# Tokens of the normalised input moved to multiples of 128 bytes, and a 272/256 split of two sections, in a hybrid decoder block on one core

## What is computed

```python
u = rmsnorm(h, norm_g[l])
proj = jnp.einsum('bld,de->ble', u, w_in[l])
hq, hf, hi, hz, aq, ak, av, az, ga, gb = jnp.split(proj, offs, axis=-1)
```

```python
yA = jnp.einsum('blw,wd->bld', oA * jax.nn.silu(hz), w_branch_a[l])
yB = jnp.einsum('blw,wd->bld', oB * jax.nn.silu(az), w_branch_b[l])
m = jax.nn.sigmoid(ga) * yA + jax.nn.sigmoid(gb) * yB
h = h + jnp.einsum('bld,de->ble', m, w_out[l])
out = rmsnorm(h, final_g)
```

## Time and profile before

| what | value |
|---|---|
| median of three executions | 758.37 us |
| the profiled execution | 758.68 us |
| its span, first to last instruction | 756.5 us |
| TensorE busy with matmuls | 737.0 us, 97% |
| VectorE busy | 462.5 us, 61% |
| ScalarE busy | 284.0 us, 38% |
| DMA traffic | 63.24 MB, mean 84 GB/s |

### The profile page before, as it was taken

The page is one execution under the profiler, slowest core; times in us unless marked ns, Lnnn a source line. Parts: engine busy times, 40 slices in busy tenths (PEclk is TensorE's granted clock), DMA queues, the critical chain, the costliest instruction groups (busy, mean ns, idle before and its releaser), DMA issues.

```text
span 756.5 us, 13114 instructions
## 1 busy us (share of the span) xinstructions
PE 737.0 (97%) x4729; PEld 656.1 (87%) x4729; DVE 462.5 (61%) x973; ACT 284.0 (38%) x580; POOL 22.9 (3%) x34
## 2 busy tenths in 40 slices
PE   3999999999999999999999999999999999999996
PEld 2998999999899899989989989998888888888885
DVE  4668669668767856966876786695643433333352
ACT  5414443542552444255145235425522222232232
POOL 2000000000000000000000000000000000000001
PEclk9999999999999999999999999999999999999999
DMA  7421220230122123023012212302323223332602
GB/s 253 126 70 56 84 84 16 68 111 28 55 83 83 55 81 85 0 83 111 28 55 83 83 33 82 107 1 85 112 85 112 83 84 111 96 98 86 246 29 111
DMA packets 105416, 63.24 MB, mean 84 GB/s; under 512 B 2067, under 2 KB 100901, under 8 KB 105397
## 3 DMA queue, kind: packets, MB, share of 16 engines
q1 hardware_dynamic: 105076, 62.33, 27.4%
q10 hardware_dynamic: 320, 0.66, 0.3%
HBM read 60.88 MB, written 2.10 MB: 83 GB/s over the span
## 4 chain that ended last, share of the span: by engine, by line
PE 96%; SPq 1%; issue 1%; DMA 1%; DVE 0%; ACT 0%; POOLq 0%; POOL 0%; DVEq 0%; ACTq 0%
PE ps L381 26%; PE ps L382 26%; PE ps L383 26%; PE ps L502 3%; PE ps L571 3%; PE ps L600 2%; PE ps L488 1%; PE ps L591 1%; PE ps L578 1%; PE ps L601 1%; PE ps L536 1%; PE ps L535 1%; PE ps L518 1%; PE ps L543 1%; DMA rows_in<-in_da_norm_g 1%
## 5 line engine op out<-in xcount | busy, mean ns | idle before, releaser
L381 PE MATMUL ps<-uT_hi,w_hi 128*128 128x512 f32 (+3 forms) x960 | 323.9, 337 | 0.0
L382 PE MATMUL ps<-uT_lo,w_hi 128*128 128x512 f32 (+3 forms) x960 | 308.6, 321 | 0.0
L383 PE MATMUL ps<-uT_hi,w_lo 128*128 128x512 f32 (+3 forms) x960 | 308.0, 321 | 0.0
L383 PEld LDWEIGHTS ps<-uT_hi,w_lo 128*128 128x128 f32 x960 | 181.0, 189 | 13.9
L381 PEld LDWEIGHTS ps<-uT_hi,w_hi 128*128 128x128 f32 x960 | 181.8, 189 | 12.1
L382 PEld LDWEIGHTS ps<-uT_lo,w_hi 128*128 128x128 f32 x960 | 181.7, 189 | 11.1
L252 DVE TENSOR_TENSOR w_lo<-w_raw,w_hi 128x1024 fp32r<-128x1024 f32 x104 | 126.2, 1220 | 95.9 <-ACT w_hi L247 95.1
L247 ACT ACTIVATE w_hi<-w_raw 128x1024 fp32r<-128x1024 f32 x104 | 110.0, 1057 | 87.5 <-PE ps L383 84.3
L809 ACT ACTIVATE e<-ps,small 128x144 f32<-128x144 f32 (+2 forms) x48 | 23.0, 483 | 47.7 <-DVE small L1194 47.7
L1140 DVE TENSOR_REDUCE small<-sq 128x4 f32<-128x512 f32 x16 | 11.0, 686 | 40.1 <-ACT sq L798 40.1
L371 POOL TENSOR_TENSOR small<-small 128x4 f32<-128x4 f32 x16 | 16.1, 1007 | 512.5 <-DVE small L1141 512.5
(11 more groups left out here) (191 smaller groups left out, 1020.4 us busy)
## 6 DMA issues: line engine op xcount, KB each, us to landing
w_raw<-in_w_in SPq DMA_DIRECT2D x80, 512.0 KB, 3.7
w_raw<-in_w_branch_a SPq DMA_DIRECT2D x8, 512.0 KB, 3.5
w_raw<-in_w_branch_b SPq DMA_DIRECT2D x8, 512.0 KB, 3.6
w_raw<-in_w_out SPq DMA_DIRECT2D x8, 512.0 KB, 3.9
x_in<-in_x SPq DMA_DIRECT2D x4, 512.0 KB, 7.8
x_res<-in_x SPq DMA_DIRECT2D x4, 512.0 KB, 6.4
out<-y_out SPq DMA_DIRECT2D x8, 256.0 KB, 2.2
rope<-in_c_rope SPq DMA_DIRECT2D x1, 528.0 KB, 6.0
```

The source lines that it names most:

```text
L381: pe.matmul(dst, w[0], rhs[0], start=start, stop=False, skip_group_check=True)
L382: pe.matmul(dst, w[0], rhs[1], start=False, stop=False, skip_group_check=True)
L383: return pe.matmul(dst, w[1], rhs[0], start=False, stop=stop, skip_group_check=True)
```

## The change

Rows of `uT_hi` and `uT_lo` become 544 floats (2176 bytes, 17 x 128): 16 floats unused, 16 meta tokens, 512 tokens. The tokens of row `k` begin at 16640 + 2176k in `uT_hi`, and at 34048 + 2176k in `uT_lo`: on a multiple of 128 bytes for each `k`, on one of 256 bytes for even `k` only. The meta tokens begin 64 bytes before. Sections 2 and 6 are cut into 272 and 256 tokens in place of 264 and 264; ScalarE takes them with two copies, of 16 and of 512 columns. The tile `z_g` is dropped, ScalarE writes the scaled gate value into `gate_a` or `gate_b`, and VectorE works there in place. The tiles behind `uT_lo` shift by 1024 bytes, those behind `z_g` by 1024 bytes the other way.

```diff
+U_AT = 2 * META
+U_PITCH = U_AT + SEQ
...
-    uT_hi, o = at("uT_hi", [P, KT, TOK], F32R, base)
-    uT_lo, o = at("uT_lo", [P, KT, TOK], F32R, o)
+    uT_hi, o = at("uT_hi", [P, KT, U_PITCH], F32R, base)
+    uT_lo, o = at("uT_lo", [P, KT, U_PITCH], F32R, o)
...
-    z_g, o = at("z_g", [P, SEQ], F32, o)
...
-    PAIR = ps[:, 0:2, 0:TOK // 2]
...
-        return walk(a[:, k, :], META + HALF + P - 1, (P, CH // 2), (-1, P))
+        return walk(a[:, k, :], U_AT + HALF + P - 1, (P, CH // 2), (-1, P))
...
-                return tuple(a[:, k, META if s == 1 else 0:META + HALF] for a in (uT_hi, uT_lo))
+                return tuple(a[:, k, U_AT if s == 1 else U_AT - META:U_AT + HALF] for a in (uT_hi, uT_lo))
...
-                            rhs = tuple(a[:, k, b * (TOK // 2):(b + 1) * (TOK // 2)] for a in (uT_hi, uT_lo))
-                            last = three(PAIR[:, b, :], w, rhs, k == 0, k == KT - 1)
+                            rhs = tuple(a[:, k, U_AT + (b * HALF or -META):U_AT + (b + 1) * HALF] for a in (uT_hi, uT_lo))
+                            last = three(ps[:, b, b * META:META + HALF], w, rhs, k == 0, k == KT - 1)
...
-                        rhs = tuple(a[:, k, META:TOK] for a in (uT_hi, uT_lo))
+                        rhs = tuple(a[:, k, U_AT:U_PITCH] for a in (uT_hi, uT_lo))
...
-                    act.activation(pair(kT[:, :]), PAIR, ACT.Copy).then_inc(sec_taken, 1)
+                    act.activation(kT[:, 0:META], ps[:, 0, 0:META], ACT.Copy)
+                    act.activation(pair(kT[:, META:]), ps[:, 0:2, META:META + HALF], ACT.Copy).then_inc(sec_taken, 1)
...
-                    act.activation(pair(vT_b[:, :]), PAIR, ACT.Copy).then_inc(sec_taken, 1)
+                    act.activation(vT_b[:, 0:META], ps[:, 0, 0:META], ACT.Copy)
+                    act.activation(pair(vT_b[:, META:]), ps[:, 0:2, META:META + HALF], ACT.Copy).then_inc(sec_taken, 1)
...
-                    act.activation(z_g[:, :], bank(2), ACT.Copy, scale=(gain_a if s == 5 else gain_b)) \
-                        .then_inc(sec_taken, 1)
+                    gate, gain = (gate_a, gain_a) if s == 5 else (gate_b, gain_b)
+                    act.activation(gate[:, :], bank(2), ACT.Copy, scale=gain).then_inc(sec_taken, 1)
...
-                    dve.scalar_tensor_tensor((gate_a, gate_b)[branch][:, :], th_z[:, :], 1.0, z_g[:, :], ALU.add,
-                                             ALU.mult).then_inc(gate_ready, 1)
+                    g = (gate_a, gate_b)[branch][:, :]
+                    dve.scalar_tensor_tensor(g, th_z[:, :], 1.0, g, ALU.add, ALU.mult).then_inc(gate_ready, 1)
```

More of the change, by code:

```diff
@@ L653, in product @@
                 last.then_inc(w_used, 1)
-            u_x = tuple(a[:, :, META:TOK] for a in (uT_hi, uT_lo))
+            u_x = tuple(a[:, :, U_AT:U_PITCH] for a in (uT_hi, uT_lo))
             branches = (oa_hi, oa_lo), (ob_hi, ob_lo)
@@ L729, in turned_x @@
                 if i == CH:
-                    act.activation(uT_hi[:, :, 0:META], bank(3)[:, 0:KT * META].rearrange("p (k t) -> p k t", k=KT),
+                    act.activation(uT_hi[:, :, U_AT - META:U_AT], bank(3)[:, 0:KT * META].rearrange("p (k t) -> p k t", k=KT),
                                    ACT.Copy).then_inc(u_ready_hi, 1)
@@ L733, in turned_x @@
                 for g in range(2):
-                    ins = act.activation(uT_hi[:, 4 * g:4 * g + 4, META + i * P:META + (i + 1) * P],
+                    ins = act.activation(uT_hi[:, 4 * g:4 * g + 4, U_AT + i * P:U_AT + (i + 1) * P],
                                          bank(4 + 2 * (i % 2) + g).rearrange("p (k t) -> p k t", k=4), ACT.Copy)
@@ L990, in turned_x @@
                 if i == CH:
-                    dve.tensor_tensor(uT_lo[:, :, 0:META], bank(3)[:, 0:KT * META].rearrange("p (k t) -> p k t", k=KT),
-                                      uT_hi[:, :, 0:META].bitcast(F32), ALU.subtract).then_inc(u_ready_lo, 1)
+                    dve.tensor_tensor(uT_lo[:, :, U_AT - META:U_AT], bank(3)[:, 0:KT * META].rearrange("p (k t) -> p k t", k=KT),
+                                      uT_hi[:, :, U_AT - META:U_AT].bitcast(F32), ALU.subtract).then_inc(u_ready_lo, 1)
                     return
                 for g in range(2):
-                    lo, hi = (a[:, 4 * g:4 * g + 4, META + i * P:META + (i + 1) * P] for a in (uT_lo, uT_hi))
+                    lo, hi = (a[:, 4 * g:4 * g + 4, U_AT + i * P:U_AT + (i + 1) * P] for a in (uT_lo, uT_hi))
                     ins = dve.tensor_tensor(lo, bank(4 + 2 * (i % 2) + g).rearrange("p (k t) -> p k t", k=4),
```

## The result

The changed kernel takes 760.09 us (median of 11), the kernel before 758.58 in the same comparison: ratio 1.002, 95% interval 1.0013 to 1.0028. It is slower by 1.5 us, a small loss that the interval sets apart from no change; 5.4 us less was forecast.

The account below looks back on a forecast made before the run. TensorE, busy 737.0 of 756.5 us, was taken as the bound. 5.1 + 1.0 - 0.7 = 5.4 us less than the profiled 758.68 gave 753.3, or 753.0 us as median; range 747.0 to 758.6.

Parts of the forecast that it names:

- The bound: Whole kernel: TensorE busy 737.0 of 756.5 us, no listed wait in the heads; each ns off a matmul shortens the end.
- The weakest step: Dense `u` stretch of the final loop: aligned rows after unaligned ones are in transition, all-aligned rows settle at `oa`'s pace.
- 512 columns: 960 matmuls on `u`: all settle as `oa` does, 5.3 ns less each, 5.1 us less; bounds 5.1 and nothing.
- Rival (a): Matmuls on `u`: only multiples of 256 or one of two phases matter; 1.1 to 2.4 us less, 756.0; chance 0.15.
- Rival (b): Matmuls on `u`: pace follows the distance between rows or hi and lo, not the address; 758.2 us; chance 0.13.
- 256 columns: 768 matmuls of the recurrence: 118.1 to 116.8 ns each, 1.0 us less; bounds 3.6 us gain, 1.6 us loss.
- The split: 768 matmuls of 264 columns become 272 and 256: 0.7 us loss; bounds 3.0 us gain, 2.0 us loss.
- ScalarE and the gate: Extra ScalarE copies (2.3 us on that engine) and the gate in place: no new TensorE wait, cost nothing.
- Rival (c): 256 and 272 pieces of `u`: fixed overhead per matmul, 256 columns at 120.2 ns, 512 stay 232.1; 762.0 us; chance 0.07.
- the rule of 16-byte lines: Rows of `u`: a start on a multiple of 64 bytes is as good as one on 128; sum would be nothing.

Follow-up runs that it names:

- e1: No layer, TensorE alone on 34 streams of 48 matmuls with varied row and weight places: 232.1 ns a matmul at pitches 2112 and 2176, 227.1 at 2304.
- e10: Kernel of e7 (rows of 2304 bytes, 264/264) with tokens 128 bytes off the weight pieces' place modulo 256: 760.10 us, ratio 1.002 to the kernel before.
- e5: No layer, 43 TensorE streams with varied places, widths and weight columns, some built as the kernel's sections: rows and weights moved together 227.5 ns a matmul.
- e2: Kernel before with only the 272/256 split of sections 2 and 6 and its copies, old pitch and gate tile: 758.57 us, ratio 0.9996.
- e4: Kernel before with only the gate made in place and z_g dropped: 758.89 us, ratio 1.0002.
- e6: Changed kernel with rows of 2304 bytes, tokens on the weight pieces' place modulo 256, og in the memory of on: 756.03 us, ratio 0.9968 to the kernel before.
- e7: As e6, with sections 2 and 6 cut at 264/264: 756.21 us, ratio 0.9965 to the kernel before.
- e12: Kernel of e7 again, on the chip of e10: 756.00 us, ratio 0.9965 to the kernel before.

## Why the prediction was wrong

- **The bound** held: TensorE at 97%, no wait in the heads, every ns of a matmul a ns of the end.
- **The weakest step failed, and it was named as such**: "I read an aligned row after an unaligned one as in transition, and a stretch of aligned rows as settled." The 5.3 ns between `u` and `oa` were real, and they do depend on addresses (e1, e10). But the modulus is 256 bytes, and it counts from the weight pieces. After the change every second row lies on their place and the others 128 off it, and the rows on the place gain nothing from it: 232.1 ns at pitch 2112 and 2176 alike (e1).
- **512 columns**, 5.1 us forecast: measured nothing, 229.33 us before and 229.40 after in sum, 11.14 for the 48 of the final loop in both. The lower bound, nothing, was the right end.
- **Rival (a)** had the modulus and the wrong outcome: it gave half of the gain for the odd rows, but three matmuls on the place between three off it gain nothing. Transition was taken as a loss of one triple, while here it is the whole stream.
- **Rival (b)** was right on the outcome for 512 columns, and in part on the reason: the distance from hi to lo matters as well (L92 of e1). Its 758.2 took the narrow pieces to be unchanged.
- **256 columns**, 1.0 us of gain forecast as the middle of 113.4 and 120.2: no such settling came. A lone stream took 117.9 at pitch 2176 against 118.3 at 2112 and 120.0 on the place (e1), and the sections of the recurrence got dearer (121.7 to 122.2, and 118.0 to 119.5, e5).
- **The split**, 0.7 us of loss forecast: 122.3 ns in the prologue against 120.8, over 768 matmuls 1.2 us; right in sign, short in size. At the old pitch it cost nothing that could be measured (e2), so the loss isn't the split's alone, as the sum had it.
- **ScalarE and the gate** at nothing held: no new wait in the profile, and e2, with the sixteen more copies, and e4 can't be told from the kernel before.
- **Rival (c)**, slower, is what happened in direction: the 512 kept their pace and the narrow pieces got dearer. Its mechanism isn't borne out: a fixed overhead showed at 256, 320 and 384 columns on the weights' place, not at pitch 2176, where 256 columns took 117.9. Its price of 3.6 us was over twice the 1.5.
- With the place right, 960 x 5.3 = 5.1 us should have come, and e6 and e7 gained 2.7 and 2.5 in their medians. In e12's profile the 960 matmuls take 226.15 us in sum against 229.33 before, 3.2 less, and the narrow ones 0.3 more. The 288 from the first `oa` on save 1.6 us, 5.5 ns each. The 648 between the prologue and there save 1.5, 2.3 ns each: among them stand the small matmuls. There the second to the seventh 512-column matmul in a row take 230.3 ns on average, 232.1 before, and those from the eighth on 226.8, 232.2 before (those right ahead of a small matmul left out). So behind each interruption the stream needs some seven matmuls to reach its pace, which was read from the traces; no run took the interruptions away. In e12's groups by shape, L382's 512-column matmuls on `uT_lo` take 391 ns on average, between 395 and the settled 389:

```profile
L382 PE MATMUL ps<-uT_lo,w_hi 128*128 128x512 f32 x320 | 125.0, 391 | 0.0
```

The prediction also weighed the rule of 16-byte lines from the Trainium skill, "SBUF — State Buffer", Specifications (TRN2). By it the sum would have been nothing, which was nearer to what came than 5.4 us less. But e10 and e12 have all rows on multiples of 64 bytes and differ by 4.1 us, which that rule doesn't explain.

## What to carry to other kernels

If two dense streams of the same shape go at different paces, compare where their rows begin relative to the weight pieces, modulo 256 bytes, and test a stream alone before moving tiles: one kernel of bare matmuls showed in one run what the trace of the layer only hinted at. For wide pieces (512 columns of `float32r`) a row pitch of a multiple of 256 on the place of the weights gave 2% of their time where nothing stood between them; for pieces of 272 and 256 in turn all places lay within 2.3 ns (121.0 to 123.3). Where a stream is interrupted every few matmuls, expect less: 2.3 ns a matmul in the heads against 5.5 in the final loop. Each of these figures is for `float32r` with a new 128 x 128 weight piece before every matmul. Reference streams must differ in one property only: `oa` was on multiples of 128 and also on the weights' place, and I took the first for the cause.

## What the hardware showed that I had not expected

- Moving only the weight pieces by 64 bytes slows a stream from 226.7 to 233.3 ns a matmul (e1), and moving both together restores it (227.5 with the transition, e5). The Trainium skill, "TensorE: Matmul & The Clock Gate", Step-by-step, says that loading the next tile's weights doesn't take read bandwidth from the running matmul. These streams differ from what that suggests: their pace depends on where the weights lie. Whether read bandwidth is the reason, no run shows.
- The best pace of 256 columns read forwards was 64 bytes off the weights' place, 113.3 ns; on it, 120.0. Read backwards, 64 off took 119.8 and on the place 118.3 (e5, L105 and L103). For 512 columns it is the other way round: 229.2 at 64 off, 226.7 on it.
- Weight pieces of 64 columns made the 512-column stream on the place slower, 230.0 ns against 226.7, and the one 128 off faster, 229.4 against 232.3 (e5).
- Inside the heads, 512-column matmuls on the weights' place reach their 226.8 ns only from about the eighth in a row on (e12); off the place they stay at 232 however long the row is (the kernel before).
